# A mixture of experts with lists of 64 slots an expert, two experts side by side, and raw fp32 weights

## What is computed

```python
def hierarchical_moe(h, w_router_group, b_router_group, w_router_expert, b_router_expert,
                     w_gate, w_up, w_down):
    t = h.shape[0]
    group_logits = jnp.matmul(h, w_router_group).astype(jnp.float32) + b_router_group.astype(jnp.float32)
    p_group = jax.nn.softmax(group_logits, axis=-1)
    g_sel = jnp.argmax(group_logits, axis=-1)
    w_grp = jnp.take_along_axis(p_group, g_sel[:, None], axis=-1)
    exp_logits = (jnp.matmul(h, w_router_expert).astype(jnp.float32)
                  + b_router_expert.astype(jnp.float32)).reshape(t, N_GROUPS, EXPERTS_PER_GROUP)
    in_group = jnp.take_along_axis(exp_logits, g_sel[:, None, None], axis=1)[:, 0]
    top_vals, top_idx = lax.top_k(in_group, TOPK_IN_GROUP)
    w_top = jax.nn.softmax(top_vals, axis=-1) * w_grp
    expert_id = g_sel[:, None] * EXPERTS_PER_GROUP + top_idx
    combine = jnp.sum(jax.nn.one_hot(expert_id, N_EXPERTS, dtype=jnp.float32) * w_top[..., None],
                      axis=1).astype(h.dtype)
    out = jnp.zeros_like(h)
    for e in range(N_EXPERTS):
        hid = jax.nn.silu(jnp.matmul(h, w_gate[e])) * jnp.matmul(h, w_up[e])
        out = out + jnp.matmul(hid, w_down[e]) * combine[:, e:e + 1]
    return out
```

## Time and profile before

| | us |
|---|---|
| median of 3 runs | 2081.21 (2075.96 to 2082.45) |
| profiled run | 2084.72 |
| its span | 2082.9 |

### The profile page before, as it was taken

How to read it: one execution, slowest core, us unless ns; L and a number is a source line. 1 busy time by engine, 2 the same in 40 slices (tenths; PEclk the granted TensorE clock), 3 DMA queues, 4 the chain that set the end, 5 groups by cost and what they waited for, 6 DMA issues and landing times. The chain is left out here.

```text
span 2082.9 us, 36838 instructions
## 1 busy us (share of the span) xinstructions
PE 1931.1 (93%) x14724; PEld 1663.9 (80%) x14724; DVE 1318.7 (63%) x2052; ACT 904.7 (43%) x1377; POOL 706.2 (34%) x381
## 2 busy tenths in 40 slices
PE   7999999997999997699999986888999999999998
PEld 4786836676777876699999866788689989999786
DVE  2677748444798897589982674566422468887413
ACT  4224238434788887522233552243342343333313
POOL 2433300241021211333445212330236555555443
PEclk9999999998999999799999897899899989999998
DMA  5222210123999998223223213210132222222231
GB/s 187 85 87 71 92 61 2 53 81 139 403 364 379 357 382 316 88 92 123 92 88 118 71 41 116 40 35 11 43 143 88 76 82 92 92 92 92 72 100 51
DMA packets 91313, 260.08 MB, mean 125 GB/s; under 512 B 26320, under 2 KB 29536, under 8 KB 90528
## 3 DMA queue, kind: packets, MB, share of 16 engines
q1 hardware_dynamic: 87424, 247.90, 33.9%
q0 software_dynamic: 3744, 10.11, 1.4%
HBM read 239.10 MB, written 18.87 MB: 124 GB/s over the span
## 5 line engine op out<-in xcount | busy, mean ns | idle before, releaser
L1755 DVE TENSOR_TENSOR moe_wlo<-moe_ring,moe_whi 128x1024 fp32r<-128x1024 f32 x198 | 233.0, 1220 | 38.7 <-ACT moe_whi L1751 37.6
L562 PE MATMUL acc<-h_xhi,h_whi 128*128 128x264 f32 x816 | 233.8, 287 | 7.0 <-DVE h_xlo L462 3.7
L562 PE MATMUL acc<-h_xhi,h_wlo 128*128 128x264 f32 x816 | 233.8, 287 | 0.0
L562 PE MATMUL acc<-h_xlo,h_whi 128*128 128x264 f32 x816 | 233.8, 287 | 0.0
L401 POOL TENSOR_TENSOR h_wlo<-ring,h_whi 128x1024 fp32r<-128x1024 f32 x59 | 142.4, 2415 | 250.6 <-ACT h_whi L392 250.3
L1751 ACT ACTIVATE moe_whi<-moe_ring 128x1024 fp32r<-128x1024 f32 x198 | 205.9, 1058 | 38.8 <-PE acc L1812 21.5
L562 PE MATMUL acc<-ff_xhi,ff_wlo 128*128 128x258 f32 x672 | 190.7, 284 | 0.0
L562 PE MATMUL acc<-ff_xhi,ff_whi 128*128 128x258 f32 x672 | 190.7, 284 | 0.0
L562 PE MATMUL acc<-ff_xlo,ff_whi 128*128 128x258 f32 x672 | 190.1, 283 | 0.0
L562 PEld LDWEIGHTS acc<-h_xhi,h_whi 128*128 128x128 f32 x816 | 155.7, 191 | 8.5 <-DVE h_xlo L462 4.1
L2322 DVE SCALAR_TENSOR_TENSOR acc<-cp,par,acc 128x528 f32<-128x528 f32 x232 | 159.4, 767 | 0.0
(11 more groups left out here) (547 smaller groups left out, 5079.4 us busy)
## 6 DMA issues: line engine op xcount, KB each, us to landing
ring<-slabs SPq DMA_DIRECT2D x213, 512.0 KB, 3.5
moe_ring<-moe_slabs SPq DMA_DIRECT2D x204, 512.0 KB, 6.2
tok_rows<-h_tok SPq DMA_DIRECT2D x5, 512.0 KB, 4.0
h_spill<-x2r SPq DMA_DIRECT2D x1, 2112.0 KB, 9.1
v_spill<-rw_v SPq DMA_DIRECT2D x1, 2112.0 KB, 7.4
y_spill<-cp SPq DMA_DIRECT2D x8, 264.0 KB, 4.6
x2r<-h_spill SPq DMA_DIRECT2D x1, 2112.0 KB, 8.8
x2r<-y_spill SPq DMA_DIRECT2D x1, 2112.0 KB, 9.8
```

Of the source, the lines that this page charges most:

```text
L562: mm = nc.tensor.matmul(acc[j][0:rows, s, 0:t1 - t0], wp[:, at:at + rows], xp[:, t0:t1], start=(k == 0 and m == 0), stop=(k == kt - 1 and ...
L1755: tensor_tensor(wlo[u % AHEAD][:, :], ringm[u % RAW][:, :], whi[u % AHEAD][:, :].bitcast(F32), ALU.subtract).then_inc(w_lo[u % 2], 1)
```

## The change

Routing now counts places for each of the 32 experts, not of the 8 groups, so a token stands in two lists. A list has 64 slots. The experts go in 16 pairs; one expert of a pair has slots and PSUM partitions 0 to 63, the other 64 to 127, and their weights stream side by side. The weights come as units of 1 MB (8 KB a partition), six for a pair, in a ring of 12, and are multiplied as they are, in fp32: no rounding, no rests. The first five units are requested at the start of the routing block, the other seven behind the stores of `tok_rows`. A pair's loop is written out 16 times and a loop stands only around passes. A slot that isn't used gets an index out of bounds and is skipped by gather and scatter (but for the first two gathers, which take row 0). A token's two results go to two planes of `moe_rows`; the entry loads both and adds them, for two tiles on VectorE and for two on GpSimd.

```diff
-MOE_AHEAD = 6
-MOE_RAW = 12
+PAIRS = N_EXP // 2
+SLOTS = P // 2
+MOE_STEPS = [("gate_up", 0)] + [step for n in range(PAIRS) for step in (("gate_up", n + 1), ("down", n)) if step[1] < PAIRS]
+MOE_UNITS = [(n, kind, i, side) for kind, n in MOE_STEPS for i in range(2 if kind == "gate_up" else 1) for side in range(2)]
+MOE_RING = 12
+UNIT = 2 * D
...
                     for t in range(4):
                         sp.dma_start(x[t][:, :], moe_d[t * P:(t + 1) * P, :]).then_inc(came[t], 16)
+                        sp.dma_start(y[t][:, :], moe_d[T1 + t * P:T1 + (t + 1) * P, :]).then_inc(came[t], 16)
...
+                    for t in range(2, 4):
+                        pool.wait_ge(came[t], 32)
+                        nc.gpsimd.tensor_tensor(y[t][:, :], y[t][:, :], x1[:, t, :], ALU.add).then_inc(second_added, 1)
                     for n in first_slabs:
                         w.pool(pool, n)
...
+                        if t < 2:
+                            dve.wait_ge(came[t], 32)
+                            L(v.tensor_tensor(y[t][:, :], y[t][:, :], x1[:, t, :], ALU.add))
+                        else:
+                            dve.wait_ge(second_added, t - 1)
+                        v.tensor_tensor(x[t][:, :], x[t][:, :], y[t][:, :], ALU.add).then_inc(added, 1)
...
                     sp.dma_start(rb[:, :], router_bias.to_broadcast([P, 40])).then_inc(biased, 16)
+                    first_units(sp, 0, 5)
                     for t in range(4):
                         sp.wait_ge(parted, 2 * t + 2)
                         sp.dma_start(tok_d[t * P:(t + 1) * P, :], h_tok[:, t, :]).then_inc(kept, 16)
-                    sp.dma_start(tok_d[T1:T1 + P, :], h_tok[:, 3, :]).then_inc(kept, 16)
-                    sp.wait_ge(kept, 80)
+                    first_units(sp, 5, MOE_RING)
+                    sp.wait_ge(kept, 64)
...
+                        def gate_up(n):
+                            for made in xt_half:
+                                pe.wait_ge(made, ps * PAIRS + n + 1)
+                            if n >= 2:
+                                pe.wait_ge(hid_made, ps * PAIRS + n - 1)
+                            for i in range(2):
+                                pair = [unit((n, "gate_up", i, side)) for side in range(2)]
+                                for q in range(4):
+                                    k = 4 * i + q
+                                    for side, (w, done) in enumerate(pair):
+                                        mm = mmul(bank(GU[n % 2])[SIDE[side], :], xts[n % 2][:, k * P + SLOTS * side:k * P + SLOTS * side + SLOTS],
+                                                  w[:, q * 512:q * 512 + 512], start=(k == 0), stop=(k == KD - 1))
+                                        if q == 3:
+                                            mm.then_inc(done, 1)
...
+                        list_slots(0)
+                        list_slots(1)
+                        turn_rows(0)
                         gate_up(0)
+                        list_slots(2)
+                        turn_rows(1)
+                        for n in range(PAIRS):
+                            if n + 1 < PAIRS:
+                                gate_up(n + 1)
+                            turn_hidden(n)
+                            if n + 3 < PAIRS:
+                                list_slots(n + 3)
+                            if n + 2 < PAIRS:
+                                turn_rows(n + 2)
+                            down(n)
...
+                        def scatter(n):
+                            for made in y_half:
+                                pool.wait_ge(made, ps * PAIRS + n + 1)
+                            pool.wait_ge(taken, ps * PAIRS + n + 1)
+                            pool.sem_inc(stepped, 1)
+                            nc.gpsimd.indirect_dma_start(moe_d, by_row(index_y[n % 5]), ys[:, :], None, bounds_check=2 * T1 - 1,
+                                                         oob_is_err=False).then_inc(put_back, 16)
+
+                        fetch(0)
+                        fetch(1)
+                        fetch(2)
+                        for n in range(PAIRS):
+                            scatter(n)
+                            if n + 3 < PAIRS:
+                                fetch(n + 3)
+                            pool.wait_ge(put_back, ps * (16 * PAIRS) + 16 * n + 16)
+                            pool.sem_inc(y_free, 1)
```

More of the change, by code:

```diff
@@ L1584, in _, with x_rows @@
                         mm.then_inc(turned, 1)
[L1586 to L1594, removed]
+                    def x_rows(i):
                         if i < 4:
@@ L1603, in _ @@
                         mm.then_inc(x_turned, 1)
+                    for i in range(4):
+                        x_rows(i)
+                    pe.wait_ge(hot_made, 1)
+                    for tok in range(4):
+                        for t in range(tok + 1):
+                            nc.tensor.matmul(acc[3][:, 1, N_EXP * tok:N_EXP * (tok + 1)], k1("before" if t == tok else "ones"),
+                                             chosen[:, t, :], start=(t == 0), stop=(t == tok))
+                    for t in range(4):
+                        mm = nc.tensor.matmul(acc[3][:, 1, 4 * N_EXP:5 * N_EXP], k1("ones"), chosen[:, t, :], start=(t == 0), stop=(t == 3))
+                    mm.then_inc(ranked, 1)
+                    for i in range(4, 8):
+                        x_rows(i)
                 @b.vector
@@ L1711, in experts @@
[L1711 to L1720, removed]
+            ringm = [mx.enter_context(nc.sbuf_tensor(f"moe_ring{j}", [P, UNIT], F32, side="right")) for j in range(MOE_RING)]
@@ L1778, in _ @@
-                    groups(sp, body)
+                    for_seam(sp)
+                    count = sp.value_load(passes[0:1, 0:1], min_val=1, max_val=T1 // SLOTS)
+                    with sp.Fori(0, count * (MOE_N // MOE_RING) - 1) as turn:
+                        chunk = (turn + 1) % (MOE_N // MOE_RING)
+                        for j in range(MOE_RING):
+                            sp.wait_ge(used[j % 2], turn * (MOE_RING // 2) + j // 2 + 1)
+                            sp.dma_start(ringm[j][:, :], moe_units[bass.ds(chunk * MOE_RING + j, 1)]
+                                         .rearrange("a p n -> (a p) n")).then_inc(unit_here[j], 16)
@@ L1829, in down @@
                             for f in range(2):
-                                hi, lo = slab(number["down", e, f])
-                                x_hi_, x_lo_ = hidt[e % 2]
                                 for half in range(2):
-                                    for m, (x, w) in enumerate(((x_hi_, hi), (x_lo_, hi), (x_hi_, lo))):
-                                        mm = mmul(bank(2 + half), x[:, f * P:(f + 1) * P], w[:, half * 512:half * 512 + 512],
-                                                  start=(e == 0 and f == 0 and m == 0), stop=(e == 3 and f == 1 and m == 2))
@@ L1849, in body @@
-                        turn_rows(n + 1)
-                        down(1)
-                        turn(3)
-                        down(2)
-                        down(3)
-                    list_slots(0, slice(0, 1))
-                    turn_rows(0)
-                    groups(pe, body)
+                                    for side, (w, done) in enumerate(pair):
+                                        mm = mmul(bank(Y[half])[SIDE[side], :], hidt[n % 2][:, f * P + SLOTS * side:f * P + SLOTS * side + SLOTS],
+                                                  w[:, f * D + half * 512:f * D + half * 512 + 512], start=(f == 0), stop=(f == 1))
+                                        if f == 1 and half == 1:
+                                            mm.then_inc(done, 1)
@@ L1986, in next_pass @@
-                    def next_pass(ps):
-                        for half in range(2):
-                            dve.wait_ge(w_lo[half], ps * (GROUPS * PER // 2) + (GROUPS * PER + AHEAD) // 2)
-                        for j in range(RAW):
-                            dve.wait_ge(slab_here[j], ps * (16 * GROUPS * PER // RAW) + 16 * (GROUPS * PER // RAW + 1))
-                        dve.wait_ge(onehot, ps * GROUPS + GROUPS + 2)
-                        nc.vector.tensor_scalar(rank[:, :, :], rank[:, :, :], -float(P), None, ALU.add).then_inc(moved_on, 1)
-                        dve.wait_ge(moved_on, ps + 1)
```

458 lines of the change are left out of this document (204 added, 254 removed).

## The result

The change made the kernel slower: 2111.12 us (median, 2105.25 to 2114.52) against 2081.83 for the kernel before, timed beside it. The ratio is 1.0135, with a 95% interval of 1.0091 to 1.0179. The forecast was 2038, the range 2024 to 2062. The profiled execution of after took 2105.25 us, that of before 2084.72.

The account below looks back on a forecast made before the run. The DMA was taken to bound the changed expert stage at 16.5 us a pair. Last expert matmul -46.4, copies out -0.5 and entry +4 sum to -43: span 2082.9 becomes 2040, median 2038, range 2024 to 2062.

Parts of the forecast that it names:

- TensorE's part: Expert stage matmuls: 0.86 us a step of both halves, 12.1 to 13.0 us a pair, no longer the bound.
- take turns: Rival at a step's two matmuls: halves run in turn, 1.72 us a step, 22.4 us a pair, 2149 us; chance 0.05.
- The DMA's part: Expert stage loads and rows: DMA becomes the bound, 16.5 us a pair at 412 GB/s, allowed 400 to 425.
- The hole at the start: DMA at the expert stage's start, after the first twelve units: a hole of 4 us.
- The chain through the gather: Expert stage, from down's copies through scatter, fetch, transposes and down: a round of 15.4 to 16.7 us, 3 us allowed.
- The first rival: Expert stage gather: landing stays at 10 to 12.3 us, round 17.4 to 19.7, total 2047 to 2080; chance 0.14.
- the second, the falling clock: Rival: TensorE's pauses lower its clock for a third of the pairs, +20 to +40 us, 2058 to 2078; chance 0.07.
- the 3 already allowed: Expert stage: 3 us in all added for the gather chain, putting the last matmul's end at 776.
- The start: Routing block's end to first expert matmul: block ends at 514.8, matmul comes 13.7 us on, at 528.5, 1.5 later.
- The seam: Expert stage's end into the entry block: copies out -0.5 us, extra loads and sums +4 (between +2 and +8).

Follow-up runs that it names:

- E1: Changed kernel with GpSimd issuing the gather of pair n+3 ahead of the scatter of pair n: 2053.29 us, ratio 0.9882 to the kernel before.
- E2: Changed kernel with the gather of pair n+3 issued only after the scatter of pair n has landed: 2186.2 us in one run.
- E3: Changed kernel with twelve matmuls of unread results ahead of each pair's row transposes, where TensorE waits for rows: 2081.8 us in one run.
- E6: E1 with all twelve first weight units requested behind the stores of token rows, none ahead: 2047.25 us, ratio 0.9811 to the kernel before.
- E5: E1 with all four entry sums of x_tok and the second plane on VectorE, none on GpSimd: 2050.46 us, ratio 0.9839 to the kernel before.
- E7: E1, E5 and E6 together in one kernel: 2043.74 us, ratio 0.9809 to the kernel before.
- E8: E1 with each 1 MB weight unit loaded by two DMAs of 4 KB a partition, as in E4: 2074.82 us in one run.
- E4: Changed kernel with each 1 MB weight unit loaded by two DMAs of 4 KB a partition: 2094.81 us in one run.

## Why the prediction was wrong

**TensorE's part was right.** A step of both halves costs 0.87 us over twelve steps in a row too (E1, 554.82 to 565.27), where 0.86 was taken from two: E1's four rounds at 12.5 us are the forecast's 12.1 to 13.0. The halves did not take turns.

**The DMA's part was right, and hidden.** 16.5 us a pair were forecast, E1 measured 16.6; 418 GB/s lie within the 400 to 425 allowed. The hole at the start was forecast at 4 us, and E1's share of 0.88 in 530 to 560, where 1.02 is full, makes 30 x 0.14 / 1.02 = 4. The place of that term in the forecast's sum, a pause from 532.1 to 536, no run shows; E1 showed in its place a share of 0.43 in 536 to 537, 0.00 in 538 to 540 and 0.86 in 540 to 542, with the first request for a freed place at 539.25, 5.7 us after the first expert matmul. In the stretches shown above a full queue moved 408 to 423 GB/s, 408 to 419 of it over 160 us.

**The chain through the gather is the step that failed.** The prediction drew the ring as it is, and put its round at 7.4 plus a landing of 8.0 to 9.3, so 15.4 to 16.7. Term by term against the round shown above:

| | forecast | after |
|---|---|---|
| copies out, start and length of the scatter, step to the fetch | 3.2 | 2.9 |
| landing, with the start of the transposes | 8.0 to 9.3 | 11.3 |
| transposes | 0.8 | 2.0 |
| down | 3.4 | 4.4 |
| round | 15.4 to 16.7 | 20.3 |

(The rows of after: 700.60 to 702.16 and 681.48 to 682.81; 682.81 to 694.13; 1.97; and 4.43. They fill this one round, 681.48 to 702.16 or 20.7 us; the mean of 13 is 20.3.) Two terms were mis-sized. First the landing, 2 to 3 us in this round and 1 to 2.4 at the median of 10.4. The value 8.0 was taken from the gather of before that was issued into a full DMA, and the argument turned on VectorE and on the size of the packets. VectorE was rightly dismissed, though it was idle in before only for the 1.2 us of that gather's instruction (its rests begin at 516.50). The instructions of 5.45 us in before ran beside four rests each (as at 575.44 to 580.06), and they account for the late landings there: 8.0 less 1.2 and 12.3 less 5.45 both leave 6.8 us. In after all 14 gathers have an instruction of 1.0 us, and 9.4 us are left. But the gather of 8.0 had no scatter ahead of it. E1 and E2, without one, measured 8.3 and 8.1; behind one it was 10.4. Why a scatter just ahead costs a gather these 2 us, no run shows. The prediction named the order of the two instructions and gave it only the 1.0 and 0.8 us of the issue. Second the clock, 1.8 us by E3. TensorE waits 4.8 to 6.3 us in a round (5.4 on average), comes back at the low level (0.50 for some 7 of the 20 us), and the transposes and the first steps of down, which lie on the ring, are paid at that level.

**The rivals were priced one by one.** The first rival, a landing of 10 to 12.3, is what happened, at the low end of its bounds, and the second, the falling clock, followed from it. Neither alone reaches the result: the first gave 2047 to 2080. The chance of 0.14 and the upper end of 2062 took the two as separate cases, though the clock fell with the wait that the landing makes (0.83 in after, 1.00 in E3, where the wait is filled). 13 rounds of 20.3 in place of 16.5 are 49 us; less the 3 already allowed, the forecast would have been near 2084. Even this count is too small, for it lets every pair cost the DMA's 16.5 from the start. With the gather off the ring the same 13 rounds took 200.6 us (E1, 560.20 to 760.79), 15.4 each, since the first four lived on units loaded ahead, where after took 264.0. These 63 us, less 4 which the pairs behind them win back, are the 59 between the ends of the last expert matmul (838.9 and 779.7): this is what the ring and its clock cost.

**The start.** 1.5 us later were forecast, it was 6.6. The stores of token rows, issued at 499.0 to 502.5 behind five units, landed 13.9 us after their issue, so that the first work of the next block came at 516.9 and not 514.8; the rest is from there to the first matmul, 16.7 us where 13.7 was taken. E6 removed 3.5 of the 6.6.

**The seam.** 34.1 us grew to 42.1, where +3.5 was forecast and +8 the upper bound. The prediction had the right rows (3.25 against 1.22) and let the two sums of GpSimd cost 0 to 4; four operations of VectorE were lengthened by 7.9 us in all where before it was two, by 2.5 (1.68 and 3.25 in place of 1.22). That and the 2.4 us of VectorE's two added sums make 7.8 of the 8.0. E5 got 3.9 back.

**Left open.** From the next block's first matmul to the end of the span, after took 3.9 us less than before, in work that the change doesn't touch. That is no gain: the same stretch took 1226.4 us in before, 1222.5 in after, 1226.9 in E1, 1217.8 in E3, 1218.3 in E7 and 1236.2 in E8. Why it varies by 18 us no run shows, but a few us between two whole times can come from it, and a difference between two kernels is safest read up to that matmul. And the median of after lies 6 us above its profiled run, that of before 3 below, so the medians (+29 us) are further apart than the spans (+20.6).

## What to carry to other kernels

When a change makes an engine idle for part of each round, look for the closed ring through its queues and sum it with the low clock in it (here 0.50 for some 7 us of a round, worth 1.8 us by E3): a bound of 20 us beside one of 16.5 is decided by such terms of 1 or 2 us. Put a fetch ahead of the store of the same round on a queue that both share, whenever its index is ready; here that was worth 2.5% of the kernel. It removed both terms at once: no wait for rows was left, and the granted clock of the stage went from 0.83 to 0.95. And requests ahead of a small transfer that others wait for are only early if the buffers they fill come free early too: here five units ahead of the stores put their landing at 13.9 us in place of 3.5, and the last expert matmul ended at 779.7 with them (E1) and at 778.2 without (E6).

## What the hardware showed that was not expected

- A gather of 128 rows landed in 8.1 to 8.3 us at the median (E2, E1) with a full DMA behind its issue, and in 10.4 us when it was issued 1.3 us behind a scatter on the same queue; the one gather issued when the last weights were almost in took 3.9 (E2).
- Pieces of 8 KB a partition moved 418 GB/s, pieces of 4 KB 408, both with a full queue over 160 us (E1, E8). With the smaller ones a gather landed 1.0 to 1.6 us sooner (7.3 in E8 against 8.3 in E1, 8.8 in E4 against 10.4 in after).
- Issuing a DMA behind many others took SyncE 1.4 us on average (14 in 19.4 us) in place of 0.6 (E8), and with a block's end waiting for SyncE this is time of the kernel (the first gather 6.7 us later than in E1).
- Operations of VectorE with two inputs of 128x1024 fp32 took 1.22 us alone and 3.25 to 3.37 us beside one of GpSimd on tiles of the same size (after, E1, E5); two that ran beside one took less, 1.68 us in before (at 833.11) and 1.22 in E5 (at 798.12).
- The instruction that issues a gather took 5.45 us beside VectorE's rests, which subtract one tile of 128x1024 from another (before), and 1.0 us without them (after).
